# Attention probabilities turned on VectorE and through DRAM, and their products with v taken two subtiles at a time

## The chip, the cores and the metric

The kernel runs on one core of one Trainium2 chip. A core has five engines that run their own instruction streams side by side: TensorE (PE), VectorE (DVE), ScalarE (ACT), GpSimd (POOL) and SyncE (SP), which here only issues DMAs. They wait for each other through semaphores. The metric is the device time of one execution in microseconds (us); less is better.

## What is computed

One layer of a decoder trunk on x of 4096 tokens by 1024 features, float32. The part that the change touches is branch C, a sliding window attention over 128 tokens with 8 query heads, 2 key/value heads and a learned sink per head:

```
h    = rms_norm(x, ln_g);  proj = h @ w_in          # u, g_pool, c_a, c_b, g_conv, q, k, v, g_attn
s    = q k^T / 8 + alibi bias, masked to the 128 keys that end at the query's own token
p    = softmax([s, sink])[..., :-1]
y_at = (p @ v) * silu(g_attn)
y    = concat(pool_mixer * silu(g_pool), conv_module * silu(g_conv), y_at)
out  = rms_norm(x + y @ w_out, final_g)
```

## The kernel before

The tokens are worked off in 8 blocks of 512 (n, `NB`), each of 4 subtiles of 128 queries (j, `SUB`). There are three stages in one program: attention (to about 617 us of the profiled execution), the pooling and convolution mixers, and the output projection. The order of the work on every engine is written out by hand, and each engine runs its list strictly in that order; nothing is scheduled by a tool.

**A block of the attention stage on PE** is `body(n)` of `tensor`: ten projections `project` of 24 matmuls each (k, q0 to q3, v, g0 to g3), every product split in three f32r matmuls (L1186, L1187, L1192). Into the second q projection after k's (q2) goes one small matmul, `fold_sums` (L276), that sums the squares of the rows of x for block n+1; it waits until these squares have been made. After v come four steps: `scores(n, j)` (L1215, L1224), then `project g_j`.

**The probabilities of a subtile** take this way. DVE reads the scores out (`take_scores`, two calls for the two kv heads: one L969, then eight instructions of L973), ACT takes the exponentials (`exps`, L842), DVE sums and inverts (`invert`, L990 and L993), POOL scales (`normalise`, L787). A row of queries has 128 keys of the window packed in 128 columns. Keys must then lie on the partitions: PE turns the eight 128x128 tiles (`turn_probs`, L1144) inside the next projection, and DVE copies them out of PSUM four times, each time times a 0/1 mask that separates the keys of the earlier and of the own tile (`pT_copy`, L1001). After that projection PE multiplies with v (`attend`, L1157, 16 matmuls for a subtile), and the result is copied to y (`output`, L1039 on DVE; L864 on ACT for subtile 2). POOL multiplies y with the gates of a whole block (`gate_output`, L796). Subtile 3 of a block is turned and multiplied in q0 of the next block; that of block 7 in the mixer's second projection, ca0 (`turn_last`, `attend_last`).

**Preparing x of the next block.** x of block n+1 is loaded by SP and ACT, two DMAs of 512 KB each (`XStage.load`, L189), as soon as DVE has made the last `split_lo` of block n (L339, semaphore `lo_done`). Its squares are summed on ACT (`square`, L239) and DVE (`square_more`, L248); then `fold_sums` on PE, `mean` on DVE, `root` on POOL, `scale` on ACT, and `turn_squares` on DVE (L301, a transpose of every 32x32 square of a 128x1024 tile, in place). In the last subtile's step DVE and ACT split the turned x into high and low parts for block n+1, four k tiles ahead of k's projection and four beside it.

**SP's queue** in a block: x, xT to DRAM in two pieces, the stores of the combined output weights (`combos`), y of the block before. At the mixer's start (`sync`, L1539 on) it waits for the last `take_scores`, loads the weights CHUNK_U, then the taps of the convolution and six small vectors (L1546, L1548), then `pw`.

## Time and profile before

| | us |
|---|---|
| median of 3 runs | 1399.58 (1399.31 to 1400.87) |
| span of the profiled execution | 1398.6 |
| PE busy in it | 1376.3 |
| DVE busy | 1189.1 |
| ACT, POOL busy | 553.6, 389.1 |

The profiled execution is about 1 us below the median. It is read so: the page says which engine is busy; the waits say where that engine stood still; the timeline, the instructions in order of time, shows how far apart two steps begin. PE's matmuls overlap, so that a duration says less than the distance between two starts: the projections' matmuls last 0.39 us and begin 0.227 us apart. The granted clock of TensorE is 0.998 of full speed (2.4 GHz) over the span.

### The profile page before, as it was taken

The page shows a single profiled execution, that of the slowest core. Times are in us where ns is not written, and L with a number is a line of the kernel's source. Part 1 is how long each engine was busy: PE and PEld are TensorE (multiplying, and loading weights), DVE is VectorE, ACT ScalarE, POOL GpSimd, SP SyncE. Part 2 cuts the span into 40 slices and gives each one's busy share as a digit, 9 for nine tenths or more (in the row PEclk, how much of TensorE's full clock was granted, in tenths as well). Part 3 has the DMA queues.
Part 4 walks back from the last instruction along what each step waited for, and adds up shares of the span by engine and source line. Part 5 has one row for each costly group of instructions (what it writes and reads, how often), then busy time and mean ns, then how long its engine had stood idle before and what let it go on. Part 6 is the DMA issues. An engine that isn't in the chain of part 4 may idle for free.

```text
span 1398.6 us, 21036 instructions
## 1 busy us (share of the span) xinstructions
PE 1376.3 (98%) x7326; PEld 1131.5 (81%) x7326; DVE 1189.1 (85%) x2480; ACT 553.6 (40%) x1435; POOL 389.1 (28%) x592
## 2 busy tenths in 40 slices
PE   6999999999999999999999999999999999999997
PEld 4888888888888888878888888888888888888886
DVE  5887878796978786769899998988999998898886
ACT  5756565655565654512212122111231333333332
POOL 5133324233242423120101101010010455445551
PEclk9999999999999999999999999999999999999999
DMA  9716070616252426363303213032326484555431
GB/s 216 206 45 257 19 273 19 235 75 207 95 199 103 151 106 210 123 118 153 136 16 136 101 66 135 15 135 101 125 113 260 201 264 161 177 180 171 159 108 74
DMA packets 89385, 197.23 MB, mean 141 GB/s; under 512 B 13904, under 2 KB 55248, under 8 KB 81616
## 3 DMA queue, kind: packets, MB, share of 16 engines
q1 hardware_dynamic: 65152, 172.28, 34.9%
q10 hardware_dynamic: 24144, 23.80, 6.5%
q8 instruction: 51, 0.84, 0.2%
q14 instruction: 38, 0.31, 0.1%
HBM read 114.27 MB, written 81.79 MB: 140 GB/s over the span
## 4 chain that ended last, share of the span: by engine, by line
PE 90%; DVE 7%; DMA 1%; ACT 1%; issue 1%; POOL 0%; SPq 0%; POOLq 0%; DVEq 0%; ACTq 0%
PE wide L346 13%; PE wide L347 13%; PE wide L348 13%; PE pair L1186 6%; PE pair L1187 6%; PE pair L1192 6%; PE wide L1186 4%; PE wide L1187 4%; PE wide L1192 4%; DVE m_tail L1967 3%; PE wide L1224 2%; PE pair L1157 2%; PE turn L1144 2%; PE turn L346 2%; PE pair L346 2%; PE pair L348 2%
## 5 line engine op out<-in xcount | busy, mean ns | idle before, releaser
L1967 DVE SCALAR_TENSOR_TENSOR m_tail<-m_tail,m_taps 128x512 f32<-128x512 f32 x480 | 338.4, 750 | 4.6
L108 POOL TENSOR_TENSOR pool_carrier<-pool_carrier 128x1 f32<-128x1 f32 x77 | 29.5, 383 | 692.0 <-DVE m_meanvar L1976 398.4
L1186 PE MATMUL pair<-xT,w_hi 128*128 128x512 f32 x384 | 154.0, 401 | 4.8 <-DVE w_lo L410 4.6
L1187 PE MATMUL pair<-xT,w_lo 128*128 128x512 f32 x384 | 150.6, 392 | 0.0
L1710 POOL TENSOR_TENSOR operand_sums<-m_y 128x512 f32<-128x512 f32 x75 | 102.0, 1360 | 167.8 <-PE wide L348 116.7
L1192 PE MATMUL pair<-xT,w_hi 128*128 128x512 f32 x384 | 147.1, 392 | 0.0
L787 POOL TENSOR_SCALAR a_rows<-a_rows,a_inv 128x128 f32<-128x128 f32 x256 | 111.4, 453 | 75.3 <-DVE a_inv L993 75.3
L346 PE MATMUL wide<-x_first,w_hi 128*128 128x512 f32 x320 | 125.5, 392 | 0.0
L346 PE MATMUL wide<-xT,w_hi 128*128 128x512 f32 x320 | 125.2, 391 | 0.0
L348 PE MATMUL wide<-x_first,w_hi 128*128 128x512 f32 x320 | 124.6, 389 | 0.0
L347 PE MATMUL wide<-x_first,w_lo 128*128 128x512 f32 x320 | 124.6, 389 | 0.0
L348 PE MATMUL wide<-xT,w_hi 128*128 128x512 f32 x320 | 124.5, 389 | 0.0
L347 PE MATMUL wide<-xT,w_lo 128*128 128x512 f32 x320 | 124.5, 389 | 0.0
L1797 ACT ACTIVATE x_first<-operand_sums 128x512 fp32r<-128x512 f32 x80 | 50.4, 632 | 154.2 <-POOL operand_sums L1710 152.5
L1186 PE MATMUL wide<-xT,w_hi 128*128 128x512 f32 x256 | 101.9, 398 | 0.0
L1192 PE MATMUL wide<-xT,w_hi 128*128 128x512 f32 x256 | 99.8, 390 | 0.0
L1187 PE MATMUL wide<-xT,w_lo 128*128 128x512 f32 x256 | 99.8, 390 | 0.0
L842 ACT ACTIVATE a_rows<-a_rows,a_negmax 128x128 f32<-128x128 f32 x256 | 98.9, 388 | 0.0
L1001 DVE TENSOR_TENSOR a_pT<-turn,a_rows 128x512 f32<-128x512 f32 x128 | 79.3, 682 | 21.8 <-PE turn L1144 21.4
L1186 PEld LDWEIGHTS pair<-xT,w_hi 128*128 128x128 f32 x384 | 72.5, 189 | 19.9 <-DVE w_lo L410 5.0
L1192 PEld LDWEIGHTS pair<-xT,w_hi 128*128 128x128 f32 x384 | 72.3, 188 | 16.0 <-DVE xT L339 0.2
L1187 PEld LDWEIGHTS pair<-xT,w_lo 128*128 128x128 f32 x384 | 72.7, 189 | 12.9
(264 smaller groups left out, 3220.0 us busy)
## 6 DMA issues: line engine op xcount, KB each, us to landing
xT_scratch<-xT SPq DMA_DIRECT2D x16, 2048.0 KB, 8.2
x_first<-xT_scratch SPq DMA_DIRECT2D x16, 1024.0 KB, 7.6
xT<-xT_scratch SPq DMA_DIRECT2D x16, 1024.0 KB, 9.0
combo_scratch<-stage SPq DMA_DIRECT2D x28, 512.0 KB, 4.4
m_y<-y_scratch ACTq DMA_DIRECT2D x14, 1024.0 KB, 6.7
xs<-in_x_dram SPq DMA_DIRECT2D x20, 512.0 KB, 8.1
y_scratch<-y_out SPq DMA_DIRECT2D x8, 1024.0 KB, 4.2
y_scratch<-y_out SPq DMA_DIRECT2D x16, 512.0 KB, 2.9
```

The costliest lines, as they stand in the source:

```text
L346: nc.tensor.matmul(out, w_hi, x_hi, start=first, stop=False)
L347: nc.tensor.matmul(out, w_lo, x_hi, start=False, stop=False)
L348: return nc.tensor.matmul(out, w_hi, x_lo, start=False, stop=last)
L787: last = nc.gpsimd.tensor_scalar(probs[:, b, h, :], probs[:, b, h, :], inv[:, b, h:h + 1], 0.5, ALU.mult, ALU.mult)
L842: last = nc.scalar.activation(probs[:, b, h, :], probs[:, b, h, :], ACT.Exp, bias=negmax[:, b, h:h + 1], accum_out=rowsum[:, b, h:h + 1])
L1001: last = nc.vector.tensor_tensor(pT[:, tile, kv, :], turn[kv][:], seen[:, tile], ALU.mult)
L1186: nc.tensor.matmul(out, w.hi(c)[:, kk, cols], st.hi[:, kk, :], start=(kk == 0), stop=False)
L1187: nc.tensor.matmul(out, w.lo(c)[:, kk, cols], st.hi[:, kk, :], start=False, stop=False)
L1192: last = nc.tensor.matmul(out, w.hi(c)[:, kk, cols], st.lo[:, kk, :], start=False, stop=(kk == KT - 1))
L1710: nc.gpsimd.tensor_tensor(operand_sums[:, i, 1], y_block(q, left), y_block(q, right), SIGN[op]).then_inc(operand_sum, 1)
L1797: nc.scalar.activation(operands[:, i, 0], operand_source(q, i), ACT.Copy).then_inc(operand_hi, 1)
L1967: nc.vector.scalar_tensor_tensor(out=conv[:, i, :], in0=h[:, i, j:j + TB], scalar=taps[:, i, j:j + 1], in1=conv[:, i, :], op0=ALU.mult, op ...
```

## The change

**Turning.** PE's `turn_probs` and DVE's `pT_copy` go. The probabilities are now kept in runs of 32 keys, the eight heads side by side in each run. DVE transposes every 32x32 square of the 128x1024 tile in place (`turn_squares_of_probs`). SP writes the tile to DRAM (`store_probs`, 512 KB) and reads it back with four DMAs of 128 KB that put each run of keys on its own 32 partitions (`load_probs`, pieces of 1 KB). There are two buffers, subtiles 0 and 2 in `whole[0]`, 1 and 3 in `whole[1]`.

**Masking.** Only half of the partitions needs a second, masked copy. POOL makes it for partitions 0 to 63 (`mask_early`), DVE for 64 to 127 (`mask_late`), two instructions of 64x512 each, and both read and write SBUF.

**Products with v.** `attend` now does two subtiles with 32 matmuls: those of subtiles 0 and 1 behind g3, the block's last gate projection, those of 2 and 3 behind v of the next block, and for block 7 behind the mixer's ca0. `output` multiplies with the gates while it reads PSUM (four instructions of 128x512 a block), so `gate_output` on POOL and the copies on ACT go.

**Order.** `turn_v` moves from scores 0 to scores 1, ACT's copy of v behind step 0. SP's list gets 5 more DMAs a subtile; where SP has to wait for `store_probs` of subtile 3, the load of x for the next block now stands behind it. At the mixer's start CHUNK_U moves behind the small vectors, and the return of subtiles 2 and 3 behind CHUNK_U. DVE's mixer work starts behind the last `output`. `square_more` uses two buffers in place of four. POOL's loop over the blocks is written out, without its carrier instructions in `normalise`.

The core of the diff:

```diff
+        def turn_squares_of_probs(m):
+            dve.wait_ge(probs_ready, 2 * m + 2)
+            nc.vector.transpose(rows[:, m % 2], rows[:, m % 2]).then_inc(squares_turned, 1)
+    def store_probs(sp, n, j):
+        m, b = SUB * n + j, j % 2
+        sp.wait_ge(squares_turned, m + 1)
+        need(sp, p_loaded[b], 16 * RUNS * (m // 2))
+        sp.dma_start(p_scratch[b], rows[:, b]).then_inc(p_stored[b], 16)
+    def load_probs(sp, n, j):
+        m, b = SUB * n + j, j % 2
+        sp.wait_ge(p_stored[b], 16 * (m // 2) + 16)
+        need(sp, pv_full, batches_before(n, j // 2))
+        squares = p_scratch[b].rearrange("(a r) (s e) -> s r a e", r=SQ, s=RUNS)
+        for s in range(RUNS):
+            sp.dma_start(whole[b][s * SQ:(s + 1) * SQ]...).then_inc(p_loaded[b], 16)
+    def mask_late(dve, n, j):                     # mask_early on POOL: the same for halves[0]
+        dve.wait_ge(p_loaded[b], 16 * RUNS * (m // 2 + 1))
+        nc.vector.tensor_tensor(runs(rest[b], halves[1]), part, over_heads(rest_mask, halves[1]), ALU.mult)
+        nc.vector.tensor_tensor(part, part, over_heads(whole_mask, halves[1]), ALU.mult).then_inc(masked, 1)
...
             else:                                 # sync, body(n)
+                load_probs(sp, n - 1, 2)
+                store_probs(sp, n - 1, 3)
                 st.load(sp, n + 1, (0, 1))
+                load_probs(sp, n - 1, 3)
...
+                take_scores(n, j, 0)              # vector, body(n)
+                if j in (1, 2):
+                    turn_squares_of_probs(SUB * n + j - 1)
+                elif j == 3:
+                    mask_late(dve, n, 1)
+                take_scores(n, j, 1)
                 invert(4 * n + j, j % 2, 0)
+                if j == 2:
+                    mask_late(dve, n, 0)
+                elif j == 3:
+                    turn_squares_of_probs(SUB * n + 2)
...
+            if not first:                         # tensor, body(n), behind v
+                attend(pe, n - 1, 1)
             for j in range(SUB):
+                scores(n, j, turn_v if j == 1 else None)
+                project(n, f"g{j}")
+            attend(pe, n, 0)
```

How it stands on the engines. On PE, before, the end of a gate projection (L1192), one subtile's products, and the next scores (L1215); `pair` and `turn` are PSUM banks:

```order
L1192 MATMUL pair<-xT,w_hi 128x512
L1157 MATMUL pair<-a_pT,a_v 64x128 [waits pT_done,a_proj_free1]
L1157 MATMUL pair<-a_pT,a_v 64x128
L1157 MATMUL turn<-a_pT,a_v 64x128 x2
L1157 MATMUL pair<-a_pT,a_v 64x128 x2
L1157 MATMUL turn<-a_pT,a_v 64x128 x2
```

On PE in the changed kernel, the end of v's projection, the products of subtiles 2 and 3 of the block before, scores 0, and the first matmul of g0:

```order
L1251 MATMUL pair<-xT,w_hi 128x512
L1214 MATMUL turn<-a_pT,a_v 64x128 [waits a_masked_early_and_late,gated,a_q_taken]
L1214 MATMUL turn<-a_pT,a_v 64x128 x7
L1214 MATMUL turn<-a_rows,a_v 64x128 x8
L1214 MATMUL turn<-a_pT,a_v 64x128 x8
L1214 MATMUL turn<-a_rows,a_v 64x128 x8
L1274 MATMUL wide<-a_k_lo,a_q 128x256 [waits score_taken]
L1274 MATMUL wide<-a_k_lo,a_q 128x256 x7
L1283 MATMUL wide<-a_k_hi,a_q 128x256 x8
L1245 MATMUL pair<-xT,w_hi 128x512 [waits a_proj_free0]
```

The products now come in one piece for two subtiles, and wait for the masked tiles instead of for DVE's copies.

On DVE, before, between the two `take_scores` of a subtile (their last instruction L979, their first L969):

```order
L979 TENSOR_TENSOR a_sinkdiff_74<-a_sinks_71,a_rowmax_72 128x4
L1001 TENSOR_TENSOR a_pT_58<-turn0,a_rows_55 128x512 [waits a_seen_ready,a_p_turned]
L1001 TENSOR_TENSOR a_pT_58<-turn0,a_rows_55 128x512
L1001 TENSOR_TENSOR a_pT_58<-turn1,a_rows_55 128x512 [waits a_seen_ready,a_p_turned]
L1001 TENSOR_TENSOR a_pT_58<-turn1,a_rows_55 128x512
L969 COPY_PREDICATED wide<-a_rows_55,wide 128x4x128 [waits score_full]
```

On DVE in the changed kernel, the same place in subtile 3 (L1039 ends the first call, L1029 begins the second; L1185 and L1186 are `mask_late` of subtile 1):

```order
L1039 TENSOR_TENSOR a_sinkdiff_74<-a_sinks_71,a_rowmax_72 128x4
L1185 TENSOR_TENSOR a_rows_55<-a_rows_55 64x512 [waits a_probs_loaded1]
L1186 TENSOR_TENSOR a_rows_55<-a_rows_55 64x512
L1029 COPY_PREDICATED wide<-a_rows_55,wide 128x4x128 [waits a_probs_stored1,score_full]
L1033 ISA a_rows_55,a_rowmax_72<-wide,a_bias_62,a_sinks_71 128x4x32 [waits a_take_step]
```

A wait for PE's turned tiles is replaced by one for DMAs that bring the tile back, with the second half of the last scores behind it.

On SP, before, from the last DMA of the attention's list (x_first) into the mixer's (m_y is where CHUNK_U and CHUNK_GC land):

```order
L542 DMA x_first<-xT_scratch 128x2048 [waits w_lo_done7]
L390 DMA m_y<-in_w_in_dram 32x8x256 [waits score_taken,score_full]
L390 DMA m_y<-in_w_in_dram 32x8x256 x3
L1546 DMA m_taps<-in_conv_dw_dram 128x31x1
L1548 DMA m_conv_bias<-in_conv_b_dram 128x1
```

On SP in the changed kernel, behind the same two taps and six vectors, which now wait for `score_taken` first (L690 stores probabilities, L699 loads them):

```order
L1582 DMA m_ln_bias<-in_conv_ln_b_dram 128x1
L1583 DMA m_pw<-in_conv_pw_dram 128x2x256
L390 DMA m_y<-in_w_in_dram 32x8x256 x4
L699 DMA a_pT<-p_scratch 32x4x256 [waits pv_full,a_probs_stored0]
L699 DMA a_pT<-p_scratch 32x4x256 x3
L690 DMA p_scratch<-a_rows 128x1024 [waits a_probs_loaded1,a_probs_squares_turned]
L699 DMA a_rows<-p_scratch 32x4x256 [waits pv_full,a_probs_stored1]
L699 DMA a_rows<-p_scratch 32x4x256 x3
```

The return of block 7's subtiles 2 and 3 (L699) has come into this list, behind the taps, the vectors and CHUNK_U; before, no product of PE waited for it.

## Rows read from the trace of the kernel before

**Rows 1.** The page: busy us, share, instructions; DMA's busy tenths in 40 slices
```profile
PE 1376.3 (98%) x7326; PEld 1131.5 (81%) x7326; DVE 1189.1 (85%) x2480; ACT 553.6 (40%) x1435; POOL 389.1 (28%) x592
...
DMA  9716070616252426363303213032326484555431
```

**Rows 2.** Waits of PE over the span: waiter, releaser, us, times, longest
```profile
PE turn L1144 <- POOL a_rows L787: 1.0, 1, 1.0
```

**Rows 3.** Timeline of PE around one subtile's turning: start, us, instruction
```profile
305.24 0.40 PE L1192 MATMUL pair<-xT,w_hi 128*128 128x512 f32 x1
305.47 1.04 PE L1144 MATMUL turn<-ident,a_rows 128*128 128x128 f32 x8
306.26 0.48 PE L1186 MATMUL pair<-xT,w_hi 128*128 128x512 f32 x1
```

**Rows 4.** Timeline of PE around one subtile's products with v, in q0
```profile
324.30 0.44 PE L1157 MATMUL pair<-a_pT,a_v 128*64 128x128 f32 x4
...
325.33 0.33 PE L1157 MATMUL pair<-a_pT,a_v 64*64 64x128 f32 x2
...
325.93 0.50 PE L1186 MATMUL wide<-xT,w_hi 128*128 128x512 f32 x1
```

**Rows 5.** Timeline of PE in block 4: the fold, and the start of scores 0
```profile
332.87 0.29 PE L276 MATMUL turn<-a_sumsq,a_fold 128*128 128x16 f32 x2
...
348.15 0.74 PE L1215 MATMUL wide<-a_k_lo,a_q 64*128 64x256 f32 x8
```

**Rows 6.** Timeline of DVE in block 4: last splits, last square, first scores, last splits
```profile
314.66 2.74 DVE L339 SCALAR_TENSOR_TENSOR xT<-xs,a_gain,xT 128x512 fp32r<-128x512 f32 x4
...
332.01 0.09 DVE L248 DVE_READ_ACCUMULATOR2_ANT a_sumsq<- 128x1 f32 x1
...
351.34 0.70 DVE L969 COPY_PREDICATED wide<-a_rows,wide 128x512 f32<-128x512 uint32 x1
...
353.44 0.69 DVE L969 COPY_PREDICATED wide<-a_rows,wide 128x512 f32<-128x512 uint32 x1
...
387.95 2.74 DVE L339 SCALAR_TENSOR_TENSOR xT<-xs,a_gain,xT 128x512 fp32r<-128x512 f32 x4
```

**Rows 7.** Timeline of SP's queue: x issued, and the first DMA that waits for x
```profile
317.43 0.87 SPq L189 DMA_DIRECT2D xs<-in_x_dram  x2
328.15 0.36 SPq L695 DMA_DIRECT2D xT_scratch<-xT  x1
```

**Rows 8.** Groups by form: DVE's transposes of squares and its copies; busy us, mean ns
```profile
L301 DVE STREAM_TRANSPOSE xs<-xs 128x1024 f32<-128x1024 f32 x28 | 34.4, 1231 | 1.5 <-ACT xs L294 1.3
L1001 DVE TENSOR_TENSOR a_pT<-turn,a_rows 128x512 f32<-128x512 f32 x128 | 79.3, 682 | 21.8 <-PE turn L1144 21.4
```

**Rows 9.** Timeline of POOL and DVE together: DVE's L488 beside POOL's L796
```profile
336.48 5.50 POOL L796 TENSOR_TENSOR y_out<-y_out,a_gate 128x512 f32<-128x512 f32 x4
...
339.42 1.40 DVE L488 TENSOR_TENSOR stage_sum<-raw 128x512 f32<-128x512 f32 x1
```

**Rows 10.** DMA issues: KB each, median us from issue to landing
```profile
y_scratch<-y_out SPq DMA_DIRECT2D x16, 512.0 KB, 2.9
out_dram<-m_tail SPq DMA_DIRECT2D x15, 512.0 KB, 4.4
out_dram<-m_tail SPq DMA_DIRECT2D x2, 256.0 KB, 2.2
```

**Rows 11.** Timeline of SP's queue at the mixer's start
```profile
605.40 1.81 SPq L390 DMA_DIRECT2D m_y<-in_w_in_dram  x4
...
607.74 7.76 SPq L1548 DMA_DIRECT2D m_conv_bias<-in_conv_b_dram  x1
...
617.19 2.42 SPq L1548 DMA_DIRECT2D m_conv_bias<-in_conv_b_dram  x1
```

**Rows 12.** Timeline of PE: scores 0 of block 7, and the mixer's first matmul of cb1
```profile
567.62 0.74 PE L1215 MATMUL wide<-a_k_lo,a_q 64*128 64x256 f32 x8
...
619.64 0.50 PE L346 MATMUL wide<-x_first,w_hi 128*128 128x512 f32 x1
```

More of the change, by code:

```diff
@@ L766, in make_seen @@
             pool.wait_ge(w.lo_done[CHUNK_Q], 2)
[L767 removed]
             nc.gpsimd.memset(earlier_tile, 1.0).then_inc(bias_step, 1)
             nc.gpsimd.memset(absent, MASKED).then_inc(bias_step, 1)
+            nc.gpsimd.memset(masks[:, 2 * P:3 * P], 1.0).then_inc(bias_step, 1)
             pool.wait_ge(bias_step, 10)
[L771 to L776 removed]
@@ L859, in body @@
                 w.split_hi(act, CHUNK_K, 1)
-            if not first:
-                act.wait_ge(proj_full, filled(n - 1, slot("o2")))
-                for late, part in enumerate(sums_of((n - 1, slot("o2")))):
-                    tokens = slice(2 * P + late * HD, 2 * P + (late + 1) * HD)
-                    last = nc.scalar.activation(y[:, :, tokens], part.rearrange("p (t c) -> p t c", t=GROUP), ACT.Copy)
-                last.then_inc(free(slot("o2")), 1)
-                if not final:
-                    st.load(act, n + 1, (2, 3))
+            if not first and not final:
+                st.load(act, n + 1, (2, 3))
             act.wait_ge(proj_full, filled(n, slot("k")))
@@ L1078, in body @@
                 make_combos(n, (t,) if t < 3 else (3, 4))
+                if t == 1 and not first:
+                    mask_late(dve, n - 1, 3)
                 if t == 2 and first:
@@ new lines, in output @@
+    def output(dve, n, batch):
+        dve.wait_ge(pv_full, batches_before(n, batch) + 1)
+        if batch == 0:
+            need(dve, y_stored, 16 * n)
+        tokens = lambda a, late: a.rearrange("p g (j l c) -> p l j g c", l=2, c=HD)[:, late, 2 * batch:2 * batch + 2]
+        for late in range(2):
+            last = nc.vector.tensor_tensor(tokens(y, late), turn[late].rearrange("p (s g c) -> p s g c", s=2, g=GROUP),
+                                           tokens(gate, late), ALU.mult)
+        last.then_inc(gated, 1)
@@ new lines, in gate_last, with attend, product @@
+    def gate_last(dve):
+        output(dve, NB - 1, 1)
+    def attend(pe, n, batch):
+        need(pe, gated, batches_before(n, batch))
+        if batch == 0:
+            pe.wait_ge(v_ready, n + 1)
+        subtiles = SUB * n + 2 * batch + 2
+        pe.wait_ge(masked, 2 * subtiles)
+        def product(s, late, kv, odd, tile, keys, start, stop):
+            out = turn[late][halves[odd], (KV * s + kv) * P:(KV * s + kv + 1) * P]
+            turned, first = (rest[s], 0) if keys is halves[late] else (whole[s], 2 * late)
+            weights = turned[keys].rearrange("p (a k t o c) -> p k o t a c", k=KV, t=2, o=2, c=SQ)[:, kv, odd, :, first:first + 2]
+            return nc.tensor.matmul(out, v[keys, 2 * batch + s + tile, halves[kv]], weights, start=start, stop=stop)
+        for s in range(2):
+            for kv in range(KV):
+                for late in range(2):
+                    for odd in range(2):
+                        product(s, late, kv, odd, late, slice(0, P), s == 0 and kv == 0, False)
+        for s in range(2):
+            for kv in range(KV):
+                for late in range(2):
+                    for odd in range(2):
+                        last = product(s, late, kv, odd, 1 - late, halves[late], False, s == 1 and kv == 1)
+        last.then_inc(pv_full, 1)
```

350 lines of the change are left out of this document (153 added, 197 removed).

## Prediction

> **What bounds the kernel now.** I read the page first, then PE's waits, then the timeline of one block in the middle. PE is busy for 1376.3 of 1398.6 us [rows 1], and of what it waits for only 1.0 us belongs to the attention's products [rows 2]. So PE's own work sets the time today: what leaves PE can be gained, and only if nothing else is late in its place. The distance to look at is that of a block. DVE ends the last splits of block 4 at 314.66 + 2.74 = 317.40 and those of block 5 at 390.69 [rows 6], 73.3 us. I call such an end L. Three steps fill it: from L to the fold of block n+1's squares at 332.87 (15.5 us), from the fold to scores 0 at 348.15 (15.3 us) [rows 5], and from there to the next L (42.5 us). In the first two PE never stops. How near the others are is seen at the fold: x of the next block is asked for at L, all of it has landed 10.7 us later [rows 7], DVE's last square ends at 332.10 [rows 6], and PE comes to the fold 0.8 us after that. That small distance is what this change runs into.
>
> **What leaves PE.** A turning starts at 305.47, and the next matmul follows at 306.26 [rows 3]: 0.79 us, and 0.1 more for the slower one behind it (0.48 in place of 0.39), 0.88. With 32 subtiles that is 28 us. The products of one subtile take 325.93 - 324.30 = 1.63 and some 0.1 of entry, 1.7; eight with 128 keys take 1.03, eight with 64 take 0.60 [rows 4]. Two subtiles in one piece have the same 32 matmuls, but enter and leave once: steady pairs of 0.215 and 0.11 give 8 x 0.215 + 8 x 0.11 = 2.6, and 0.4 for the edges, 3.0 in place of 3.4. In 16 pieces some 7 us. Together 35 us, 4.4 a block, are the most that can be gained. The new moving operand is read in runs of 32 columns, which no row shows; I take it at the old speed.
>
> **What PE then waits for: the fold.** Between L and the fold PE loses the turning in q0 and one subtile's products, 2.6 us, and would be there at L + 12.9. The squares are not: even at their old time they are done at L + 14.8. And x comes later. On SP its load now stands behind `store_probs` of subtile 3, whose transpose DVE makes only after L, 1.2 us [rows 8], so SP's half starts some 1.9 us late and with 0.5 MB of probabilities ahead of it. The four loads were 2.1 MB in 10.7 us, of which I take 3 as fixed, 0.27 MB a us; 0.5 MB more is 1.9 us. ACT's half starts on time, so I count 1.7, not both. x is there at L + 12.4; ACT's eight squares then take 3.2, which makes the fold L + 15.6, between 14.8 (nothing is late) and 17 (both delays). So PE waits some 2.7 us there in each of blocks 1 to 6.
>
> **From the fold to scores 0** PE has the same 15.3 and the 3.0 of the two subtiles' products: 18.3.
>
> **From scores 0 to L** DVE's list decides, as it did: it begins its first scores 3.2 us behind PE's [rows 5, 6] and ends with L. Removed: three `pT_copy` groups of four at 0.60 apart, 7.2, and two `output` pairs, 1.3 (0.682 is the duration of one copy, [rows 8]; they overlap by a little). The start comes earlier by 1.55, since the products behind v give DVE time to finish what is late today; its new `output` (1.3) is in that figure. Added: three transposes of 1.2 [rows 8], 3.6; `mask_late` of subtile 0 beside other work of POOL, 1.3. `mask_late` of subtile 1 is the costly one. It has two instructions that read and write SBUF, and POOL starts its own two at the same moment, since both wait for the same DMAs. The row to go by is DVE's L488, 1.40 us beside POOL's gating, where an instruction of this shape with one operand in PSUM takes 0.68 [rows 8, 9]. Between 1.3 and 2.8 I take 2.2. Behind it wait the second call of the last `take_scores` and all eight splits.
> It also has to wait for the DMAs. A store of 512 KB lands after 2.9 to 4.4 us, 3.5; the four loads are issued 0.45 apart, and the last lands 2.2 to 2.6 after its issue, 3.9 [rows 10, 11]; with SP's wake-ups 7.5 us. Between the end of subtile 1's transpose and `mask_late` DVE has two calls of 2.1 [rows 6], two `invert` of 0.3, a mask of 1.3 and a gate of 0.6: 6.7. So 0.8 are waited for (0 to 2.5). Sum: 42.5 - 1.55 - 7.2 - 1.3 + 3.6 + 1.3 + 2.2 + 0.8 = 40.4.
>
> The skill has a rule that speaks against the two masks side by side: the Trainium skill, "SBUF — State Buffer", on the shared port pair, says that a DVE instruction with two SBUF inputs and a GpSimd one that reads SBUF exclude each other for their whole length. With that rule taken word for word `mask_late` could cost up to two of POOL's instructions more, an estimate of 1.3 + 2 x 1.3 = 3.9, and a block 1.7 more than in my sum; the 1.40 of L488 [rows 9] is what this trace shows of it, a wait for part of one.
>
> **The block.** 15.6 + 18.3 + 40.4 = 74.3 us, against 73.3. PE's 4.4 us are gone and 1.0 more: the circle L, x, squares, fold, scores, DVE, L is longer than PE's work, so it sets the pace. It goes round 6 times (blocks 1 to 6): +6.0, between 6 x (71.5 - 73.3) = -11 and 6 x (77 - 73.3) = +22. At its short end stand no late x (14.8), no wait and no conflict (38.5), and products at 2.9.
>
> **Block 0** has no fold behind an L and begins its scores as today; it gains what DVE gains, 42.5 - 40.4: -2.1 (0 to -4).
>
> **Block 7 and the change of stage.** There is no fold. From L to scores 0 the turning (0.9) goes and the products grow by 1.3: +0.4. Then, before, from scores 0 at 567.62 to the end of subtile 3's products, where cb1 starts at 619.64 [rows 12], PE took 52.0 us with no wait. Now the last two subtiles must come back from DRAM through SP's list. With S as scores 0: `take_scores` was all done at S + 37.7, just before SP's first row [rows 11]; by the items above and 0.2 of start it comes to 37.7 + 0.2 - 7.2 - 1.3 + 2.4 + 1.3 + 2.2 = S + 35. DVE transposes subtile 2 (1.2 + 0.3), SP stores it at S + 36.4 and turns to the taps and vectors. Their DMAs are of 4 bytes an element, and SP stood 7.76 and 2.42 us at the one behind each taps load, the first time also behind 1 MB of CHUNK_U [rows 11]. Without that I take 2.4 twice and seven issues of 0.44: 7.9, S + 44.3. CHUNK_U takes 1.8 [rows 11], the load of subtile 2 1.8, so the store of subtile 3 goes out at S + 48, behind 1.75 MB in its queue, and lands at S + 54; the load 4.0, S + 58; POOL's two masks of 1.3 S + 60.6; products 3.0: S + 63.6. PE has nothing else to do: it comes there at about S + 45 (29.4 for the four steps, 2 of wait for the masks of subtile 1, 3.0 for products, 10.9 for cb0 and ca0). So it waits 15 us, and the stage is 63.6 - 52.0 = 11.6 longer (8 to 15). All of the mixer is behind it: DVE's first mixer step waits for the same products, so it hides nothing.
>
> **Sum** against the profiled execution: -2.1 + 6.0 + 0.4 + 11.6 = +15.9, 1398.6 + 15.9 = 1414.5. The median stands 1 us above that span, which gives 1415.5; I say 1415. What else changes costs nothing: POOL has 389 busy us of 1399 and its gating goes (5.5 a block, [rows 9]) where eight masks a block come, ACT loses copies, `square_more` keeps its pace, since with two buffers an instruction waits for the one two before it, which ended. The 32 MB more of DMA lie where the DMA engines are busy for 3 to 4 tenths on average over the attention's slices [rows 1], but for the places named.
>
> **The rivals.**
> Faster: the circle closes sooner. The place is `mask_late` of subtile 1 and the load of x. If the tile is back before DVE asks for it, DVE and POOL take turns without loss, and ACT's half of x carries the fold, a block takes 71.5 us: -11 - 4 + 8.4 = -6.6, about 1392. It decides from 73.0 us a block down: there the loss at the change of stage is no longer covered. For it: three of its terms have no row of their own. Against: the fold's 0.8 us cannot be argued away, PE arrives 2.6 earlier. Chance 0.16.
> All of it gained: no wait at the fold nor at the change of stage, so PE stays the bound: 1398.6 - 35 = 1363. Every term above speaks against it. 0.04.
> No net change: the circle stays at 73.3 and SP's small loads are quick (the taps 1 us each), so that the stage loses only 4: about 1400 to 1402. 0.10.
> Clearly slower: queues. If a store and a load of probabilities take 10 us together, as x does [rows 7], `mask_late` waits 3.3 and x comes 2 later: 78 us a block, +28, with 12 + 4 at the end: 1440. For it: x too comes in pieces of 1 KB. 0.12.
> My forecast holds the rest, 0.58.
>
> **The range.** The forecast's own bounds run from 1396 to 1432. With half of the faster and of the far slower case left out: 1395 to 1434. A difference of 0.2%, 2.8 us, is about what a measurement can tell here. Faster 0.20, the same 0.10, slower 0.70.
>
> **What would show it.** After: in PE's waits a row of L276 (fold) on the squares' producer or on DMA, 15 to 20 us over six times, and a row of `attend` (L1214) of 10 to 18 us once, with some 1 to 2 us in each block. No L1144. A distance of 74 us between ends of the last splits. `mask_late` at 0.7 to 1.4 an instruction in subtile 3's step. On SP the store of the last tile 12 us behind the taps. I am wrong if PE has no row for the fold, if blocks are below 73 us, or if the last products follow ca0 within 8 us.

## Result: 1462.7 us against 1400.2, slower by 4.5%

The changed kernel takes 1462.7 us (median of four runs, 1462.4 to 1464.8), the kernel before 1400.2 us (1399.3 to 1400.9): a ratio of 1.0447, interval 1.0433 to 1.0462. The forecast was 1415, in a range from 1395 to 1434. The direction was right, the size was not: +62.5 us where +15 was expected. The profiled execution of the changed kernel has a span of 1463.1 us against 1398.6; it is the slowest of the four.

The page of the changed kernel, busy time by engine and TensorE's granted clock in 40 slices (compare [rows 1]; before, the mean granted clock was 0.998, here it is 0.974):

```profile
PE 1365.0 (93%) x7070; PEld 1121.5 (77%) x7070; DVE 1214.7 (83%) x2429; ACT 549.5 (38%) x1421; POOL 436.2 (30%) x576
...
PEclk9999999999999989997999999999999999999999
```

PE's waits over the span (waiter, releaser, us in total, times, longest). [Rows 2] had 1.0 us of POOL's here and no row for the fold:

```profile
PE turn L276 <- ACT a_tanh L239: 34.3, 6, 6.5
PE turn L1214 <- POOL a_rows L855: 27.8, 7, 17.6
PE wide L1274 <- DVE a_rowmax L1033: 10.0, 8, 1.6
```

L276 is the fold, L1214 the products with v, L1274 the scores. PE stood still for 22.3 us before (1398.6 - 1376.3) and for 98.1 now, 75.8 more.

One block in the middle, on SP, ACT and PE, in that order. L is 337.60 here; compare [rows 5, 7]:

```profile
339.50 0.34 SPq L690 DMA_DIRECT2D p_scratch<-a_rows  x1
339.88 1.25 SPq L189 DMA_DIRECT2D xs<-in_x_dram  x2
...
351.98 0.42 ACT L239 ACTIVATE a_tanh<-xs 128x256 f32<-128x256 f32 x1 [4.91 <-DMA xs<-in_x_dram]
...
355.54 0.58 PE L276 MATMUL turn<-a_sumsq,a_fold 128*128 128x16 f32 x2 [5.12 <-ACT a_tanh L239]
...
372.91 1.09 PE L1214 MATMUL turn<-a_pT,a_v 128*64 128x128 f32 x16
...
375.84 0.73 PE L1274 MATMUL wide<-a_k_lo,a_q 64*128 64x256 f32 x8
```

SP issues x 2.3 us behind L instead of at L. x is there at L + 14.4 (L + 10.7 before), and PE has stood at the fold for 5.1 us when ACT's squares are done. The products of two subtiles take 375.84 - 372.91 = 2.9 us, as forecast.

To see all six blocks at once I read three distances of each block from the timelines: from L to the fold, from there to scores 0 (S), and to the next L. These are means over blocks 1 to 6, in us, for every kernel of this study. They come from the one profiled execution of each, which can lie off its median: e1's is 3.5 us below it, e4's 3.0 below, e3's 3.6 above, the changed kernel's 2.1 above. So a difference of half a us a block between two rows says little:

```
                                    L-fold  fold-S  S-L   block
forecast                             15.6    18.3   40.4   74.3
before                               15.5    15.3   42.5   73.3
after                                18.5    20.8   41.3   80.6
e1  x first on SP                    15.4    19.0   41.2   75.6
e2  a quarter of the trip's bytes    17.4    20.7   42.9   81.0
e3  the stop at the fold filled      19.1    18.6   41.1   78.8
e4  fold in q3                       18.5    18.2   41.6   78.3
e5  trip first at the change         18.4    20.8   41.5   80.7
e6  e1, e4 and e5                    18.3    14.7   42.2   75.1
e7  before, fold in q1               14.9    23.1   42.5   80.5
e8  masks on POOL                    19.1    20.5   40.5   80.1
e10 e6, products behind scores 0     18.1    10.3   45.7   74.1
e11 e10, others behind k             21.3    11.2   45.4   78.0
e12 e11 with the fold in q2          20.6    17.5   44.8   82.9
e13 masks on DVE                     18.4    20.7   41.3   80.5
e14 e10 with masks on DVE            18.1    11.0   45.3   74.5
```

In e10, e11, e12 and e14 the distances hold other work, since products were moved over S or L; only the block can be compared there.

**Where the 64.5 us of the span came from.** Block 0: its L is at 96.06 instead of 97.53, -1.5. Six blocks: the distance from the first to the last L is 483.8 instead of 439.6, +44.3. From L to scores 0 in block 7, 31.6 instead of 30.5: +1.1. The change of stage, from scores 0 of block 7 to cb1, 684.43 - 611.54 = 72.9 against 52.0 [rows 12]: +20.9. From cb1 to the end 778.7 against 779.0: -0.3.

The change of stage, on SP, POOL and PE:

```profile
649.33 0.34 SPq L690 DMA_DIRECT2D p_scratch<-a_rows  x1
649.76 0.38 SPq L1580 DMA_DIRECT2D m_taps<-in_conv_dw_dram  x1
650.20 3.62 SPq L1582 DMA_DIRECT2D m_conv_bias<-in_conv_b_dram  x1
...
659.37 1.95 SPq L390 DMA_DIRECT2D m_y<-in_w_in_dram  x4
661.41 1.82 SPq L699 DMA_DIRECT2D a_pT<-p_scratch  x4
663.33 0.38 SPq L690 DMA_DIRECT2D p_scratch<-a_rows  x1
670.78 1.73 SPq L699 DMA_DIRECT2D a_rows<-p_scratch  x4
...
675.60 1.76 POOL L854 TENSOR_TENSOR a_rows<-a_rows 64x512 f32<-64x512 f32 x1 [2.46 <-DMA a_rows<-p_scratch]
677.33 1.70 POOL L855 TENSOR_TENSOR a_rows<-a_rows 64x512 f32<-64x512 f32 x1
...
679.18 1.98 PE L1214 MATMUL turn<-a_pT,a_v 128*64 128x128 f32 x16 [17.64 <-POOL a_rows L855]
680.91 1.95 PE L1214 MATMUL turn<-a_rows,a_v 128*64 128x128 f32 x16
```

The last tile is stored 13.6 us behind the taps, needs 7.5 us to land and comes back at S + 64. And the last products take 5.25 us, not 2.9: 16 of them need 1.98 where they took 1.09 in the middle of the kernel.

### The profile page after: what moved, and what is told of

Its sections match the earlier page's. It is cut to its first block, busy times and chain, and to the rows that moved or that the text cites. A ratio compares the mean times of both kernels' runs of the same rounds, so it can differ in the third digit from the quotient of the medians.

```text
span 1463.1 us, 20591 instructions
## 1 busy us (share of the span) xinstructions
PE 1365.0 (93%) x7070; PEld 1121.5 (77%) x7070; DVE 1214.7 (83%) x2429; ACT 549.5 (38%) x1421; POOL 436.2 (30%) x576
## 4 chain that ended last, share of the span: by engine, by line
PE 67%; DVE 13%; DMA 10%; ACT 3%; SPq 2%; issue 2%; POOL 2%; POOLq 0%; ACTq 0%; DVEq 0%
PE wide L346 12%; PE wide L348 12%; PE wide L347 12%; DMA xs<-in_x_dram 5%; PE pair L1245 3%; PE pair L1246 3%; PE pair L1251 3%; DVE m_tail L2004 3%; DMA a_rows<-p_scratch 2%; PE wide L1245 2%; PE wide L1246 2%; PE wide L1251 2%; DVE a_rows L1058 2%; PE turn L1214 2%; PE pair L348 2%
## 5 line engine op out<-in xcount | busy, mean ns | idle before, releaser
L845 POOL TENSOR_SCALAR a_rows<-a_rows,a_inv 128x128 f32<-128x128 f32 x256 | 117.1, 476 | 253.1 <-DVE a_inv L1053 253.1
L108 POOL TENSOR_TENSOR pool_carrier<-pool_carrier 128x1 f32<-128x1 f32 x23 | 14.1, 611 | 395.1 <-DVE m_meanvar L2013 395.1
L346 PE MATMUL wide<-xT,w_hi 128*128 128x512 f32 x320 | 125.2, 391 | 0.0
L348 PE MATMUL wide<-xT,w_hi 128*128 128x512 f32 x320 | 124.5, 389 | 0.0
L347 PE MATMUL wide<-xT,w_lo 128*128 128x512 f32 x320 | 124.5, 389 | 0.0
L1245 PE MATMUL wide<-xT,w_hi 128*128 128x512 f32 x256 | 106.9, 418 | 0.0
L1246 PE MATMUL wide<-xT,w_lo 128*128 128x512 f32 x256 | 104.7, 409 | 0.0
L1251 PE MATMUL wide<-xT,w_hi 128*128 128x512 f32 x256 | 104.6, 409 | 0.0
L1246 PEld LDWEIGHTS pair<-xT,w_lo 128*128 128x128 f32 x384 | 72.9, 190 | 13.7
L1033 DVE CUSTOM_DVE_ANT_0 a_rows<-wide,a_bias,a_sinks 128x128 f32<-128x128 f32 x256 | 74.6, 349 | 2.3
```

What stands on the lines that cost most here:

```text
L346: nc.tensor.matmul(out, w_hi, x_hi, start=first, stop=False)
L347: nc.tensor.matmul(out, w_lo, x_hi, start=False, stop=False)
L348: return nc.tensor.matmul(out, w_hi, x_lo, start=False, stop=last)
L845: last = nc.gpsimd.tensor_scalar(probs[b][:, h], probs[b][:, h], inv[:, b, h:h + 1], 0.5, ALU.mult, ALU.mult)
L1033: last = nc.vector.tensor_tensor_reduce(out=probs[b][:, h], in0=in_runs(score[:, h, P:]), in1=in_runs(bias[:, h]), scale=1.0, scalar=sinks ...
L1245: nc.tensor.matmul(out, w.hi(c)[:, kk, cols], st.hi[:, kk, :], start=(kk == 0), stop=False)
```

## Experiments

### Is it the order on SP? (e1, e2)

e1 exchanges two lines of SP's list:

```diff
                 load_probs(sp, n - 1, 2)
-                store_probs(sp, n - 1, 3)
                 st.load(sp, n + 1, (0, 1))
+                store_probs(sp, n - 1, 3)
                 load_probs(sp, n - 1, 3)
```

> The changed kernel with one change: on SP the load of the next block's x stands ahead of the store of subtile 3's probabilities instead of behind it. In the changed kernel x has landed 14.4 us after the end of the last splits (L) and PE waits 5.7 us at the fold in each of six blocks. Theory: the order on SP costs the 2.3 us from L to SP's issue. Then SP issues x at L + 0.1, it has landed at L + 12 to 12.5, the fold comes at L + 15.6 to 16, and the waits at the fold fall from 34.3 to some 21 us; with the clock that comes back 2.2 to 2.8 us a block, 1446 to 1450 us. Rival: the amount of data in the queues decides, not the order: x lands at L + 14 as now, 1460 to 1463 us.

Measured: 1436.9 us, ratio 1.0269 (1.0252 to 1.0286), 26 us less than the changed kernel. SP's queue, and PE's wait at the fold (in this run L is 324.00):

```profile
324.03 0.85 SPq L189 DMA_DIRECT2D xs<-in_x_dram  x2
325.89 0.34 SPq L690 DMA_DIRECT2D p_scratch<-a_rows  x1
```
```profile
PE turn L276 <- ACT a_tanh L239: 15.3, 6, 3.2
```

The first square on x starts at 335.7, L + 11.7. The theory holds, and the gain is larger than the 2.2 to 2.8 us a block that I gave it: 5.0 between the two profiled executions, 4.3 by the medians (25.8 / 6). Of the 5.0, 3.1 are the distance to the fold, 1.8 lie behind the fold: in four of six blocks fold to S is 18.3, just the forecast.

e2 leaves the order alone and takes away three quarters of the bytes (the rest of what the products read is then stale, so this kernel's output is not the layer's):

```diff
-        sp.dma_start(p_scratch[b], rows[:, b]).then_inc(p_stored[b], 16)
+        sp.dma_start(p_scratch[b][0:SQ], rows[0:SQ, b]).then_inc(p_stored[b], 16)
...
-            sp.dma_start(whole[b][...].rearrange("r (a e) -> r a e", a=RUNS), squares[s]
+            sp.dma_start(whole[b][...].rearrange("r (a e) -> r a e", a=RUNS)[:, 0:1], squares[s][:, 0:1]
```

> The changed kernel, but of each tile of probabilities only a quarter makes the trip (32 of 128 rows stored, one of four runs of 1 KB a row loaded back; the rest of what the products read is stale, so the attention's result is not the reference's). Every wait and every issue stays. It tells the bytes from the order on SP, which the run with x first has shown to be worth 5.0 us a block. Theory: order and wake-ups made x late, not bytes: x still starts 2.3 us behind L on SP, and lands at L + 13, the fold comes at L + 16.5, 1.4 us sooner than with all bytes; with the clock 2 to 2.5 a block, and 2 to 4 us at the change of stage: 1444 to 1450 us. Rival: the bytes decide: x lands at L + 11.5 as with x first, and the last stores land 4 us sooner: 1425 to 1432 us.

Measured: 1463.4 us, 1.0458 (1.0440 to 1.0475): no gain at all, but as the sum of two effects. The fold comes 1.2 us sooner (17.4 instead of 18.5), so of the 3.1 us that e1 won about this much is bytes, and the change of stage is 68.0 us instead of 72.9 (from scores 0 of block 7 at 614.25 to cb1 at 682.21), 4.9 less. But S to L is 1.6 us longer, which neither theory had and which takes most of this back. DVE's small instructions of `take_scores` (L1039, 128 x 4 elements) show why. Groups of the blocks, after and e2: busy us and mean ns, then e2's timeline of DVE and POOL in block 4:

```profile
L1039 DVE TENSOR_TENSOR a_sinkdiff<-a_sinks,a_rowmax 128x4 f32<-128x4 f32 x49 | 8.7, 177 | 0.0
```
```profile
L1039 DVE TENSOR_TENSOR a_sinkdiff<-a_sinks,a_rowmax 128x4 f32<-128x4 f32 x48 | 20.3, 423 | 0.0
```
```profile
398.29 1.28 POOL L854 TENSOR_TENSOR a_pT<-a_pT,a_rows 64x512 f32<-64x512 f32 x1
...
398.65 0.94 DVE L1038 TENSOR_SCALAR a_negmax<-a_rowmax 128x4 f32<-128x4 f32 x1
399.51 1.33 DVE L1039 TENSOR_TENSOR a_sinkdiff<-a_sinks,a_rowmax 128x4 f32<-128x4 f32 x1
399.54 1.28 POOL L855 TENSOR_TENSOR a_pT<-a_pT,a_rows 64x512 f32<-64x512 f32 x1
```

The tile comes back sooner, so POOL's masks start in the middle of DVE's list, and an instruction of 0.15 us takes 1.33, as long as a mask. L1038, which reads one tile only, is held as well (0.94 instead of 0.17). Of the 128 instructions of these two lines in a whole execution, 9 take 0.7 us or more in the changed kernel (seven of them L1038) and 31 in e2, every one of them beside a mask of POOL; in the kernel before and in e13 below, where POOL makes no masks, none takes more than 0.17.

### What does a stop of PE cost? (e3, e7)

e3 fills PE's stop with work that nobody needs:

```diff
                 if kk == (4 if n == 0 else 1):
+                    if n > 0:
+                        for i in range(24):
+                            nc.tensor.matmul(q_bank(3), w.hi(CHUNK_Q)[:, i % KT, 0:P], st.hi[:, i % KT, :],
+                                             start=True, stop=True)
                     need(pe, gated, batches_before(n, 0) - 1)
```

> The changed kernel with 24 matmuls of 512 columns whose result nobody reads (5.1 us) put in front of PE's wait at the fold in blocks 1 to 6, in the place of the 5.7 us in which it stands still. Theory: the stop costs more than its length, since the granted clock is lower behind it (0.83 to 0.87 in its stretch of 20 us, 0.91 to 0.98 in the next), some 2 to 2.5 us a block. Then the extra work makes the kernel faster, by 12 to 15 us: 1448 to 1451 us, with a granted clock of 0.98 or more in the blocks and a distance from fold to scores 0 of 18.2 to 18.5 instead of 20.3. Rival: the longer distances are DMA traffic or waits, and the clock is only a symptom: 1463 to 1466 us.

Measured: 1449.8 us, 1.0354 (1.0337 to 1.0372). 144 matmuls more, and 13 us less. The theory's time and its distance hold: from fold to S it is 18.6 instead of 20.8. PE in the 2.5 us behind the fold of block 4, after and then e3 (us, PE busy with the number of matmuls, granted clock, DMA share, GB/s), and e3's wait at the fold:

```profile
355.50:358.00 2.50, 2.46 (x7) 0.50 0.94 402
```
```profile
348.10:350.60 2.50, 2.50 (x13) 1.00 0.91 387
```
```profile
PE turn L276 <- ACT a_tanh L239: 3.1, 2, 2.0
```

DMA is as busy in both, so it isn't traffic that slows PE behind the fold. It is the clock: a granted clock of 1.00 is 2.4 GHz, 0.50 is 1.2, and at 0.50 PE gets through 7 matmuls where it otherwise does 13.

e7 makes such a stop in the kernel before, with nothing of the change in it, by asking for the fold one projection earlier:

```diff
-project(n, name, folding(n) if name == ("q3" if first else "q2") and not final else None)
+project(n, name, folding(n) if name == ("q3" if first else "q1") and not final else None)
```

> The kernel before with one change: the fold of the next block's squares stands in the projection q1 instead of q2 in blocks 1 to 6, 5.1 us earlier in PE's order. The squares end at L + 14.7 as before, so PE, which comes to the fold at L + 10.4, must wait some 4.3 us there, with nothing else changed. Theory: a stop costs its length and some 2 us of lower clock behind it: 6 x (4.3 + 2.2) = 39, 1439 us, granted clock down by 0.01 to 0.02 in the mean. Rival: it costs its length alone: 6 x 4.3 = 26, 1426 us, and the clock stays at 0.998.

Measured: 1442.7 us, 1.0310 (1.0293 to 1.0327), 42.7 us more. Its waits at the fold, and PE in the 6.4 us behind one of them (the fold starts at 353.56):

```profile
PE turn L276 <- DVE a_sumsq L248: 23.2, 5, 4.6
...
PE turn L276 <- ACT a_tanh L239: 5.1, 1, 5.1
```
```profile
353.60:360.00 6.40, 6.40 (x18) 0.56 0.65 230
```

The kernel before has 42 matmuls in the same 6.4 us of its own trace, at a granted clock of 1.00. The stops of e7 are 28.3 us long together and cost 42.8 of span (1441.4 - 1398.6). The 14.5 between them are 2.4 us for each stop of 4.7, and PE, which has the same matmuls, is busy for 15.4 us more (1391.7 - 1376.3), so it is the lower clock. S to L stays at 42.5. The rival that a stop costs its length alone falls. The step that my sum did not have is this one: PE arrives early, waits, and then works more slowly for a while.

The other side of it is in e1. There the stops were 2.6 us on average, and in four of six blocks nothing was lost behind them. The price does not follow the length alone: the longest of them, 3.2 us (block 1), cost nothing more, one of 3.1 (block 2) cost 2.7 and one of 2.3 (block 3) 1.6. What decides it between 2 and 3.2 us no run here shows.

### The change of stage (e5)

```diff
         sp.wait_ge(score_taken, ATTENDED)
+        attention.turn_loads(sp)
+        w.load(sp, CHUNK_U)
         with nc.allow_non_contiguous_dma(reason="per-channel constants, once"):
...
         sp.dma_start(pw[:], conv_pw[0].rearrange("(i p) d -> p i d", p=P)).then_inc(small_loaded, 16)
-        w.load(sp, CHUNK_U)
-        attention.turn_loads(sp)
         w.load(sp, CHUNK_GC)
```

> The changed kernel with another order of SP's loads at the change of stage: the return of the last two subtiles' probabilities first, then CHUNK_U, then the taps, the vectors and pw. Theory: PE's wait of 17.6 us in front of the last products is the time that SP spends on the small loads (S + 38 to S + 48) and on CHUNK_U. Then the last tile is stored some 5 us behind the products of subtiles 0 and 1 and is back at S + 48, the last products start at S + 52 instead of S + 67.6, and PE waits 0 to 3 us: 15 to 18 us less, 1445 to 1448 us. Rival: the weights and taps that now come 10 us later hold up the mixer's first tile by as much (PE waits for them instead): 1458 to 1463 us.

Measured: 1450.2 us, 1.0357 (1.0340 to 1.0375), 12.5 less. From scores 0 of block 7 (609.75) to cb1 (669.77) it is 60.0 us instead of 72.9:

```profile
650.59 2.01 SPq L699 DMA_DIRECT2D a_pT<-p_scratch  x4
652.69 0.38 SPq L690 DMA_DIRECT2D p_scratch<-a_rows  x1
656.23 1.74 SPq L699 DMA_DIRECT2D a_rows<-p_scratch  x4
658.01 1.91 SPq L390 DMA_DIRECT2D m_y<-in_w_in_dram  x4
...
664.82 1.97 PE L1214 MATMUL turn<-a_pT,a_v 128*64 128x128 f32 x16 [5.10 <-POOL a_rows L855]
```

That is 2 us above the theory's 1445 to 1448. SP's small loads and CHUNK_U were the cause of most of the wait, but 5.1 us of it are left, which is the trip itself, and the products behind it are as slow as before. The taps, now asked for at S + 50 instead of S + 38, cost nothing that I could find: 778.6 us from cb1 to the end.

### Asking later (e4, e6)

e4 moves the fold into q3 and DVE's reading of it with it:

```diff
-project(n, name, folding(n) if name == ("q3" if first else "q2") and not final else None)
+project(n, name, folding(n) if name == "q3" and not final else None)
...
-                if t == 1 and not first and not final:
+                if t == 2 and not first and not final:
                     st.mean(dve, n + 1)
```

> The changed kernel with the fold of the next block's squares one projection later on PE (in q3 instead of q2, 5.1 us), and DVE's reading of its result moved with it, in blocks 1 to 6. Theory: the wait at the fold is a matter of where PE asks: 34.3 us shrink to 0 to 5, the clock stays up, and what hangs on the fold (root, scales, transposes of x) has slack until the next L; then a block is shorter by 5.1 + 2.0: -43, 1418 to 1423 us. Rival: DVE or ACT becomes late by what the fold gives up, since both have the mean, four scales and three transposes of x to do before the scores, so PE waits for DVE in front of the products or the scores: a block is shorter by 2 to 4 only, 1438 to 1450 us.

Measured: 1449.7 us, 1.0360 (1.0343 to 1.0377): the rival. PE's wait at the fold has gone to the products:

```profile
PE turn L1214 <- POOL a_rows L855: 27.6, 6, 19.0
PE turn L1214 <- DVE a_q L1078: 23.3, 7, 4.4
...
PE turn L276 <- ACT a_tanh L239: 1.0, 1, 1.0
```

a_q is `make_q_lo`, which now stands on DVE behind the mean and a transpose of x. A block is only 2.4 us shorter.

e6 puts e1, e4 and e5 together.

> The changed kernel with three moves together: x first on SP, the fold in q3, the trip ahead of the small loads at the change of stage. Theory: no stop is left in a block, so from L to scores 0 PE needs its work alone: 12.9 to the fold's old place + 15.3 + 3.0 = 31.2, and from there to L 40.4 to 41.7: 71.6 to 72.9 a block against 73.3 before. Six blocks give -10 to -2, block 0 -1.5, the change of stage + 8 (S + 60.1 to cb1 as measured with the trip first, against 52.0): 1395 to 1403 us. Rival: DVE's list from scores 0 to L grows by what it could not do earlier, and blocks stay at 75 as with x first alone: 1415 to 1420 us.

Measured: 1418.6 us, 1.0141 (1.0119 to 1.0163): 44 of the 62 us are gone, and the time lies in the rival's 1415 to 1420. Blocks are 75.1, 0.5 less than with x first alone; by the medians it is some 1.0 (18.3 us less than e1, of which e5 explains 12.5). The fold's place was worth little once x was on time, well below the 2.4 us a block of e4.

### Who owns the distance from scores 0 to L? (e8, e13, e10 to e14)

e8 gives POOL both halves of every mask, e13 gives both to DVE. e13 does in `mask_late` what e8 does in `mask_early`. This is e8's edit; the calls of `mask_late` are also taken out of DVE's list, and POOL waits for its own instructions before (some of these waits are left out here):

```diff
+            part = runs(whole[b][:, D // 2:], halves[1])
+            pool.wait_ge(masked, 2 * m + 1)
...
+            nc.gpsimd.tensor_tensor(runs(rest[b], halves[1]), part, over_heads(rest_mask, halves[1]), ALU.mult)
+            nc.gpsimd.tensor_tensor(part, part, over_heads(whole_mask, halves[1]), ALU.mult).then_inc(masked, 1)
```

> The changed kernel with all masks of returned probabilities on POOL, both halves of a tile, none on DVE. Theory: DVE's two masks of subtile 1 (0.69 + 1.79 us, and 0.3 of wait) and of subtile 0 (1.3) stand in the list that leads from scores 0 to L, so this distance falls from 41.7 by some 3 us to 38.5; POOL, alone on the port, takes 1.28 each. Six blocks give 18 us back, and the last masks at the change of stage cost 1.5 to 2 more: 1445 to 1449 us. Rival: POOL then ends the masks of subtile 1 2.5 us later (four in a row behind its normalising), the products of subtiles 0 and 1 wait for them, and L, which comes behind PE's last projection, is not earlier: 1460 to 1475 us.

Measured: 1463.7 us, 1.0450 (1.0422 to 1.0477): no gain, as the rival had it. S to L is 0.8 shorter, but L to the fold is 0.6 longer, and PE waits longer for POOL in front of the products, 44.6 us in all instead of 27.8.

> The changed kernel with all masks on DVE, both halves of a tile, none on POOL: the opposite of the run with all masks on POOL. Theory: the two engines take turns at the port, so what POOL did beside DVE was no help: DVE's four masks of a tile take 0.69 each, 2.8, where its two took 2.5 beside POOL (0.69 + 1.79), and the small instructions of its list (L1038, L1039: 0.26 and 0.18 on average, up to 1.3) go back to 0.17. From scores 0 to L then +0.3 for subtile 1, +1.4 for subtile 0, -1.1 for the collision: 41.3 becomes 41.9; the masks at the change of stage are done 0.7 sooner each: 1461 to 1467 us. Rival: POOL's half is real help, and DVE's list grows by 2 x 1.4 in this distance: 44.1, six times 2.8, 1478 to 1482 us.

Measured: 1461.3 us, 1.0430 (1.0412 to 1.0447), and S to L is 41.3 in every block, what it was with POOL's help. The groups of DVE in the blocks, first after, then e13 (busy us, mean ns):

```profile
L1186 DVE TENSOR_TENSOR a_rows<-a_rows 64x512 f32<-64x512 f32 x12 | 19.2, 1601 | 0.0
...
L1185 DVE TENSOR_TENSOR a_rows<-a_rows 64x512 f32<-64x512 f32 x12 | 12.2, 1013 | 2.6 <-DMA a_rows<-p_scratch 2.5
```
```profile
L1178 DVE TENSOR_TENSOR a_rows<-a_rows 64x512 f32<-64x512 f32 x12 | 8.2, 684 | 0.0
L1180 DVE TENSOR_TENSOR a_rows<-a_rows 64x512 f32<-64x512 f32 x12 | 8.2, 683 | 0.4
```

Two masks on DVE beside POOL's took 1.01 + 1.60 = 2.6 us, four on DVE alone take 4 x 0.68 = 2.7. POOL's half bought nothing. The Trainium skill, "SBUF — State Buffer", section "Who interferes with whom", calls it "an exclusive lock": a DVE instruction with two SBUF inputs and a GpSimd one that reads SBUF don't overlap. e13's sum agrees. The 1.33 us of a 128 x 4 instruction in e2 are this rule too, and they show what my sum left out: the small instructions of DVE's list can be held up, not only the masks, and the traces show it for L1038 as well, which has one SBUF input.

e10 takes e6 and lets PE come later to what it waited for: the products of subtiles 2 and 3 behind scores 0, a scale of ACT and a transpose of DVE behind q3's, the last products behind cb1:

```diff
-            if not first:
-                attend(pe, n - 1, 1)
...
                 scores(n, j, turn_v if j == 1 else None)
+                if j == 0 and not first:
+                    attend(pe, n - 1, 1)
                 project(n, f"g{j}")
```

> The kernel with three moves (x first, fold in q3, trip first) and three more: the products of subtiles 2 and 3 behind scores 0 of the next block instead of behind v; on ACT the second scale behind q_hi(3), on DVE the first transpose of x behind q_lo(3); the last products behind cb1 instead of ca0. In the run with three moves PE still waited in a block 1.4 us for q_lo, 0.9 for POOL's masks of subtile 3 and for DVE's last output in front of the products (distance fold to scores 0 of 14.7 on average, 12.8 at best), and 5.1 us in front of the last products, as long as cb1 takes. Theory: what these steps wait for is ready 2 to 3 us later at no cost: blocks fall from 75.1 to 72.5 or 73, the change of stage by 4 to 5: 1397 to 1404 us. Rival: S to L is DVE's list and its length is what counts, so that a later output lengthens it by as much: 1412 to 1416 us.

Measured: 1411.8 us, 1.0084 (1.0068 to 1.0101), at the rival's 1412 to 1416 and far from the theory's 1397 to 1404. Blocks are 74.1, so that S(7) is 1.1 us ahead of the kernel before (566.49 against 567.62). The last products wait for 0.3 us only, but 3.4 for DVE's m_sums and 1.5 for its y_out come in their place. Since DVE's mixer begins with the gating of these products, cb1 was no cover for it.

e11 moves the products of subtiles 0 and 1 behind the next k projection as well, with x ahead of the return of subtile 2 on SP; e12 is e11 with the fold and what hangs on it back in q2.

> As the run before it in this list, and the products of subtiles 0 and 1 behind the next block's k projection instead of behind the last gate projection, with x ahead of subtile 2's return on SP. In the run with three moves PE waits 2.8 us in front of these products for POOL's masks of subtile 1 (1.77 + 1.75 us beside DVE's), and the clock falls behind it. Theory: behind k the masks are long done, and PE has no wait of more than 1.5 us left in a block: 70 to 72 a block, which with the change of stage some 5 above before and block 0 at -1.5 gives 1378 to 1394 us, faster than before. Rival: L is DVE's end and DVE's list from scores 0 to L is the circle's longest part (40.4 to 42), so an earlier PE only waits elsewhere, for the splits in k or the scores: 1396 to 1405 us.

> As the run before it, but with the fold in q2 and ACT's and DVE's scales and transposes of x where the changed kernel has them. It tells what the place of the fold is worth when the products of subtiles 0 and 1 (3.0 us) stand between L and the fold: PE comes to q2's fold 3.0 us later, at L + 15.9, where x first alone had the squares ready at L + 15.3. Theory: then the fold needs no move: no wait at L276, within 3 us of the run with the fold in q3. Rival: SP's x is late again, since x, two loads and a store crowd behind L, and the fold waits 2 us or more: 12 us or more slower than with the fold in q3.

Measured: 1443.8 us, 1.0302 (1.0284 to 1.0320), and 1470.8 us, 1.0499 (1.0481 to 1.0516). e11 misses both of its ranges, though its rival's mechanism is there: PE waits for the splits. Of e12 the rival has the sign, a fold that waits 4.6 us a block and 27 us more than e11, but not the reason. PE's waits in e11:

```profile
PE pair L1250 <- DVE xT L339: 16.1, 24, 2.8
PE wide L1273 <- DVE a_q L1077: 11.1, 7, 3.3
```

S to L stays at 45.4 (45.7 in e10) although 3.0 us of products left it, so in e10 it seems to be DVE's list, not PE's work, that ends it, and PE waits for the splits instead; the products then lengthen L to S, where PE is the bound. In e12 x is asked for at L and ACT's squares of it start at L + 12.6, but DVE's squares stand behind `mask_late` of subtile 2, and that waits for a load which is now issued 3.6 us behind L, with x ahead of it in the queue, and is there at L + 14.3: the mask ends at 358.9, the first square starts there, and the last ends at L + 20.5.

> The kernel with the products behind scores 0 (1411.8 us, 74.1 us a block) and all masks on DVE. There the masks of subtile 1 took 1.74 + 1.68 on DVE beside POOL, 3.4, and PE waited 7.8 us in all for POOL's masks. Theory (turns at the port): 2.8 in place of 3.4 and no wait for POOL, against 1.4 more for subtile 0 and 2.8 more for subtiles 2 and 3 where DVE has time: a block stays at 74 or becomes 73.5, and the last masks are done 0.7 to 1.4 sooner: 1406 to 1412 us. Rival (POOL's half is help, DVE's list is the circle): a block is longer by 2 to 2.8: 1424 to 1429 us.

Measured: 1412.6 us, 1.0084 (1.0068 to 1.0101), as e10. The theory of turns at the port holds once more; the contention is not what keeps the repaired kernel above the one before.

No version beat the kernel before. What keeps e10 above it is 0.8 us a block, and above all what follows scores 0 of block 7, with the change of stage in it: 841.7 us from there to the end against 831.0.

## Why the forecast was too low

The sum in the forecast had the right places, and a block and a stage that were each too short: 74.3 against 80.6, and 63.6 against 72.9.

- **What leaves PE** was forecast as 35 us at most. e10 has the same matmuls as the changed kernel and a granted clock of 0.995, and is busy for 1351.6 us against 1376.3: 25 us. So the 64.5 us are 75.8 more of standing still, 24.7 less of work and 13.4 of the same work at the lower clock (1365.0 - 1351.6).
- **x at the fold: the term that was too small.** I counted 1.7 us for x's delay, "not both" of the late start and the bytes ahead, and took 15.6. It was 18.5. In block 4 x was there at L + 14.4, 3.7 later than before and not 1.7. (The forecast's bound of 17 for both delays was itself low: its own terms, 10.7 + 1.9 + 1.9 + 3.2, give 17.7.) The late start was 2.3 instead of 1.9, since DVE's transpose itself waited 0.6 for POOL's normalising. e1 shows 3.1 us for the order as a whole, and e2 1.2 for three quarters of the bytes. With x first the fold is at L + 15.4, near the forecast's number, but with x there at L + 11.7, 1.0 late, where the forecast had 1.7 with the order as it was. 18 us of the miss are in this term.
- **Fold to scores 0: the term that was missing.** 15.3 + 3.0 is right when PE doesn't stop (18.6 in e3, 18.3 in four blocks of e1). Behind a stop of 5.7 it was 20.8. 2.5 us, six times, 15 us. I priced every wait at its length; e3 and e7 show that a stop of this length costs about half as much again, at the lower clock.
- **Scores 0 to L**: 40.4 against 41.3. The trip took 397.96 to 405.08, 7.1 us (7.5 forecast), and `mask_late` of subtile 1 with its wait 2.8 (3.0 forecast). Beside them stands L1039 in block 4 (in most other blocks L1038), 1.28 us instead of 0.15 where POOL's mask of subtile 0 meets it, which is 1.1. The two masks side by side took 0.69 + 1.79 = 2.5, near the 2.2 that I took and far from the 3.9 of the strictest reading; the mistake was to look for the turns at the masks alone. 5 us.
- **Block 0 and L to S of block 7**: -1.5 and +1.1, forecast -2.1 and +0.4.
- **The change of stage**: +20.9 instead of +11.6. The chain was the one forecast; its links were longer. The last tile is stored at S + 51.8 (48), since DVE was done 1.2 later and SP's small loads took 9.6 us instead of 7.9. Its store landed after 7.5 (6), the load came back after 4.8 (4.0), the masks took 3.4 (2.6), and the products 5.25 (3.0), because PE had stood for 17.6 us and its clock was down to 0.59 in the stretch from 660 to 680. 9 us of the miss are here. That everything of the mixer is behind this point was right.
- **The rivals.** "Queues" had the nearest price for a block, 78, but its mechanism, a trip of 10 us, did not come; the trip was 7.1. What came was x 2 us later, one of its two delays, and the clock, which none of them had.
- **The signs.** No L1144, a wait of 17.6 at L1214 once and 1.7 a block, masks of 0.7 to 1.8, the last tile 13.6 behind the taps: as listed or a little beyond. L276 at 34.3 instead of 15 to 20, and 80.6 between L's, were the two that showed the miss.

What stays open: why e10's blocks are 0.8 us above those of the kernel before, where PE's work is 3 us shorter. e11 points to DVE's list as the limit there, but no run made that list shorter.

## What to carry to other kernels

When a step leaves the engine that is the bound, that engine comes early to the next wait: write down what it will wait for there, and who issues that load behind what. A stop of some 5 us of TensorE costs its length and about half as much again, so a cheap transfer that makes it wait can cost more than the matmuls it replaced. And when DVE and POOL both work on SBUF, count the work of both in one sum.

## What I had not expected of the hardware

- The granted clock after a stop: 144 useless matmuls in the stops made the kernel 13 us faster (e3). Stops of 4.7 us cost 2.4 more each (e7); of stops of 2.0 to 3.2 us, four of six cost nothing more, the longest among them (e1).
- A DVE instruction on 128 x 4 elements took 1.33 us instead of 0.15 beside POOL's mask (e2), so that an earlier landing of data made S to L 1.6 us longer.
- Two masks on DVE beside two on POOL took as long as four on DVE (e13), and 0.69 became 1.79.
- A tile of 512 KB through DRAM and back took 7.1 us in a block. With a quarter of its bytes the kernel took the same time: what the earlier landing won at the fold and at the change of stage, DVE lost beside POOL's masks (e2).
